# MoE routing inside a two-layer encoder: slot lists from eight one-hot products, the slot table written behind the first gathers, router products inside the output projection

## The chip, the cores and the metric

The kernel runs on one core of one Trainium2 chip. The metric is the device time of one execution in microseconds (us), median of several executions; lower is better. TensorE (PE) does the matrix products, VectorE (DVE) the elementwise work and reductions, ScalarE (ACT) activations and copies, GpSimd (POOL) some elementwise work and all indexed transfers, SyncE (SP) issues the weight transfers. The engines run side by side and wait for one another on semaphores.

## What is computed

Two layers, each a token mixer followed by a mixture of experts (MoE) on 512 tokens of width 1024. Layer 0's mixer is windowed attention, layer 1's a gated DeltaNet; the change touches only what follows the mixer. The MoE picks one of 4 groups and then the best 2 of its 8 experts for every token:

```python
g_logits = (t @ w_group) + b_group
g_prob, g_idx = lax.top_k(jax.nn.softmax(g_logits, axis=-1), 1)
e_logits = ((t @ w_expert) + b_expert).reshape(-1, N_GROUPS, EXPERTS_PER_GROUP)
e_sel = jnp.take_along_axis(e_logits, g_idx[:, :, None], axis=1)[:, 0]
e_prob, e_idx = lax.top_k(jax.nn.softmax(e_sel, axis=-1), TOP_K)
gate = g_prob * e_prob / jnp.sum(e_prob, axis=-1, keepdims=True)
...
hid = jax.nn.silu(jnp.einsum('td,edf->tef', t, w_gate)) * jnp.einsum('td,edf->tef', t, w_up)
hid = hid * combine[..., None].astype(hid.dtype)
return jnp.einsum('tef,efd->td', hid, w_down).reshape(B, S, D)
```

All is float32. An expert's three matrices are 1 MB each, 3 MB per expert, 32 experts per layer.

## The kernel before

Tokens are cut into four tiles (`TT = 4`) of 128. Every engine runs one program written out by hand; its order is the order of the calls, and semaphores tie the engines together. Around the change, in each layer:

- **Output projection** (`project_back_pe/dve/act`): for each token tile two half-width sums of 24 products (`three`), added to `x` by DVE (L315). DVE, ACT and POOL then normalise the tile (ACT L223, DVE L238, POOL L229, DVE L241 into `hn`); PE turns it (L251, `turn_pe`) so that channels lie on partitions, and ACT and DVE copy the turned tile to `ht` (L263, L277). The turn of tile t-1 stands between the two halves of tile t; that of the last tile follows the last half.
- **Router products** (`moe_pe`, L842): for all four tiles, one after another, eight products each of the tile with 36 router columns. An f32 product is two instructions, so 64 instructions in all. They begin when the last turn is done.
- **Choice** (`moe_dve`): DVE waits for the products and for `pool_c`, adds the bias (L981), and finds group and two experts by a chain of small operations that each wait for the one before (`first_max`, L972 to L977, three times). The result is two one-hot arrays `oh`. PE turns them into each token's rank within its expert (L847 to L854).
- **Table and slot lists**: DVE works out each token's row in a table in DRAM (`pos_i`, L997 to L1004). POOL writes 1,024 entries of 8 bytes there with eight indexed transfers (L738), waits until all have landed, and reads the first 64 slots of each of the 32 experts back (L743). PE turns what came (L859, L861) and DVE makes the integer lists `idx_i` from it (L1016, L1018).
- **Experts**: POOL gathers 64 token rows of an expert with one indexed transfer (L753), eight ahead (`AHEAD = 8`); PE turns them (L867), multiplies with gate and up (L875) and later with down (L884); DVE makes `hidden` (L1029) and copies the result (L1025), POOL scatters it (L760). Expert weights go through a ring of three slots (`RING = 3`) that SP refills: gate and up of a slot when L875 of its expert is done (L1924), down when L884 is (L1932).
- **POOL's own preparation** (`moe_pool`): after the four stores of `hn` to `h_rows` (L717) it writes constants (six iotas, L719 to L726) and clears the eight gather buffers (L729); the last clear raises `pool_c`. In layer 0 `masks_pool` follows, which waits until the stores of `h_rows` have landed before its last two iotas (L632, L633). DVE has a counterpart, `masks_dve`, in layer 0.

If an expert has more than 64 tokens, `late_passes` takes the rest from the table. The branch is decided at run time.

## Time and profile before

| | us |
|---|---|
| median of 3 runs | 1538.74 |
| lowest, highest | 1535.88, 1540.78 |
| span of the profiled execution | 1541.2 |
| PE busy, share of the span | 1245.0, 81% |
| PE weight loads (PEld) | 919.6, 60% |
| DVE / POOL / ACT busy | 625.7 / 508.5 / 381.3 |

The page cuts the span in 40 slices of 38.5 us and gives for each the busy share in tenths, the clock that TensorE was granted (in tenths of full speed) and the bytes moved. The two long stretches with the transfers at 9 are the expert loops of the layers. The rows farther below are from the trace of one execution, with times from the start of its span; a matmul row such as "L842 ... x64, 13.71" is a run of 64 instructions that took 13.71 us from the start of the first to the end of the last.

### The profile page before, as it was taken

Reading aid. Unit: us, or ns where it says so; the run is one execution under the profiler, and the core shown is the slowest. Engines: PE = TensorE matmul, PEld = TensorE weight load, DVE = VectorE, ACT = ScalarE, POOL = GpSimd, SP = SyncE. Lnnn points to the kernel's source line nnn. Section 1 sums busy time; section 2 is a strip of 40 time slices with the busy share of each in tenths; the row PEclk is TensorE's granted clock in tenths of the full one; section 3 lists DMA queues with packets and bytes.
Section 4 is the critical chain, followed back from the end, with each engine's and each line's share of the span. In section 5 each row is a group of like instructions: output and inputs, shape, how many; then the busy total and the mean of one; then the engine's idle time right before and its main releaser. Section 6 shows DMA issues by size and latency. Waiting matters only on the chain. (4 is left out here: it accounts for less than half of the span.)

```text
span 1541.2 us, 19154 instructions
## 1 busy us (share of the span) xinstructions
PE 1245.0 (81%) x7501; PEld 919.6 (60%) x7501; DVE 625.7 (41%) x1202; ACT 381.3 (25%) x796; POOL 508.5 (33%) x472
## 2 busy tenths in 40 slices
PE   5999989459887784798789988889979458888883
PEld 4776677435544452576688866678868434545451
DVE  4447642401111114477775576775282201111113
ACT  3325531011010012253433334332331011010010
POOL 1321000422222211045886355985440432222210
PEclk8999999579999997799999999999989579999997
DMA  6201001549999997011000130000321559999995
GB/s 207 77 34 55 1 21 60 214 167 382 396 398 387 394 411 303 0 55 55 1 1 1 55 109 2 1 1 1 110 69 55 218 190 386 404 398 392 388 408 218
DMA packets 66219, 270.65 MB, mean 176 GB/s; under 512 B 17133, under 2 KB 17389, under 8 KB 41553
## 3 DMA queue, kind: packets, MB, share of 16 engines
q1 hardware_dynamic: 52048, 246.25, 41.4%
q0 software_dynamic: 12064, 21.32, 4.1%
q10 hardware_dynamic: 2016, 1.84, 0.4%
q8 instruction: 62, 1.02, 0.3%
q14 instruction: 29, 0.23, 0.0%
HBM read 262.78 MB, written 23.35 MB: 186 GB/s over the span
## 5 line engine op out<-in xcount | busy, mean ns | idle before, releaser
L875 PE MATMUL bank<-ring,arena 128*64 128x256 f32 x2048 | 261.1, 408 | 73.6 <-issue 73.1
L875 PEld LDWEIGHTS bank<-ring,arena 128*64 128x64 f32 x2048 | 168.0, 141 | 147.7 <-issue 88.3
L760 POOL DMA_INDIRECT y_rows<-arena,idx_i x64 | 64.1, 1002 | 406.0 <-DVE arena L1025 391.2
L1318 PE MATMUL bank<-arena 128*128 128x128 f32 x1088 | 141.5, 287 | 14.9 <-DVE arena L1824 7.5
L1029 DVE TENSOR_TENSOR arena<-arena,bank 128x128 f32<-128x128 f32 x64 | 18.4, 287 | 326.8 <-ACT arena L952 321.6
L1318 PEld LDWEIGHTS bank<-arena 128*128 128x128 f32 x1088 | 132.9, 199 | 27.3 <-DVE arena L1824 11.6
L884 PE MATMUL bank<-ring,arena 128*64 128x512 f32 x512 | 123.9, 604 | 1.5 <-DVE arena L1034 1.5
L952 ACT ACTIVATE arena<-bank 128x128 f32<-128x128 f32 x64 | 17.7, 277 | 424.0 <-PE bank L875 381.3
L148 PE MATMUL bank<-ring_r,ht_r 128*128 128x512 f32 x288 | 113.5, 394 | 0.0
L1025 DVE COPY arena<-bank 128x512 f32<-128x512 f32 x64 | 44.3, 692 | 144.5 <-PE bank L884 144.5
L146 PE MATMUL bank<-ring_r,arena_r 128*128 128x512 f32 (+1 forms) x228 | 91.8, 403 | 3.4 <-DVE ring_r L170 3.4
L251 PE MATMUL bank<-ident,hn 128*128 128x128 f32 x192 | 38.5, 370 | 64.4 <-DVE hn L241 49.8
L147 PE MATMUL bank<-ring_r,arena_r 128*128 128x512 f32 x224 | 88.5, 395 | 0.0
L170 POOL TENSOR_TENSOR ring_r<-ring,ring_r 128x1024 fp32r<-128x1024 f32 x32 | 80.1, 2524 | 24.5 <-ACT ring_r L164 24.5
L867 PEld LDWEIGHTS bank<-ident,arena 64*128 64x128 f32 x512 | 61.3, 202 | 34.6 <-issue 25.1
L147 PE MATMUL bank<-ht_r,ring_r 128*128 128x512 f32 x192 | 77.9, 406 | 0.0
L867 PE MATMUL bank<-ident,arena 64*128 64x64 f32 x512 | 70.1, 278 | 9.3 <-DMA arena<-h_rows,idx_i 9.3
L251 PEld LDWEIGHTS bank<-ident,hn 128*128 128x128 f32 x192 | 33.0, 210 | 70.5 <-DVE hn L241 44.0
L1716 DVE SCALAR_TENSOR_TENSOR arena<-arena 128x512 f32<-128x512 f32 x72 | 72.8, 1011 | 2.6
L753 POOL DMA_INDIRECT arena<-h_rows,idx_i x64 | 60.7, 948 | 25.7 <-issue 18.9
L229 POOL TENSOR_TENSOR norm_s<-norm_s,mhalf 128x1 f32<-128x1 f32 x16 | 8.9, 555 | 178.1 <-DVE norm_s L238 178.1
L1629 POOL TENSOR_TENSOR arena<-ring,arena 128x512 f32<-128x512 f32 x48 | 61.9, 1310 | 6.9 <-PE bank L1318 6.9
(284 smaller groups left out, 2215.8 us busy)
## 6 DMA issues: line engine op xcount, KB each, us to landing
ring<-in_moe_w_gate SPq DMA_DIRECT2D x64, 1024.0 KB
ring<-in_moe_w_up SPq DMA_DIRECT2D x64, 1024.0 KB
ring<-in_moe_w_down SPq DMA_DIRECT2D x64, 1024.0 KB
ring<-in_gdn_w_in SPq DMA_DIRECT2D x8, 2048.0 KB
arena<-y_rows SPq DMA_DIRECT2D x16, 512.0 KB, 7.3
ring<-in_attn_w_in SPq DMA_DIRECT2D x3, 2048.0 KB
ring<-in_attn_w_out SPq DMA_DIRECT2D x2, 2048.0 KB
h_rows<-hn POOLq DMA_DIRECT2D x8, 512.0 KB, 13.9
```

The lines of the kernel that those rows point to most:

```text
L146: pe.matmul(dst, a[0], b[0], start=start, stop=False)
L147: pe.matmul(dst, a[0], b[1], start=False, stop=False)
L148: return pe.matmul(dst, a[1], b[0], start=False, stop=stop)
L170: eng.tensor_tensor(panel(n, False, True)[:, c, :], panel(n)[:, c, :], panel(n, True, True)[:, c, :].bitcast(F32), ALU.subtract).then_inc( ...
L251: last = pe.transpose(b[:, j * P:(j + 1) * P], hn[:, t, half * 4 + j::KC], ident[:, :])
L760: pool.indirect_dma_start(out=y_rows[l], out_offset=bass.IndirectOffsetOnAxis(ap=idx_i[:, 1, e:e + 1], axis=0), in_=y_out[:, e % RING, :], ...
L867: last = pe.transpose(bank[0][:, c * SLOTS:(c + 1) * SLOTS], xg[0:SLOTS, i, c::KC], ident[0:SLOTS, 0:SLOTS])
L875: last = pe.matmul(bank[1][m * SLOTS:(m + 1) * SLOTS, 0:2 * P].rearrange("p (w n) -> p w n", w=2), xgt[:, i, c * SLOTS:(c + 1) * SLOTS], w ...
L884: last = pe.matmul(bank[3][half * SLOTS:(half + 1) * SLOTS, :], hidden_t[:, i, m * SLOTS:(m + 1) * SLOTS], d[:, m, half * HALF:(half + 1) ...
L1318: last = pe.matmul(bank[b][:, h * P:(h + 1) * P], lhs(h), rhs(h), start=True, stop=True)
L1629: pool.tensor_tensor(lm[slot], lt_of(n), by_head(level[l]), ALU.mult).then_inc(g["lm"], 1)
L1716: last = dve.scalar_tensor_tensor(out=acc, in0=u_pad[:, U % 2, k:k + SEQ], scalar=conv_w[:, at:at + 1], in1=acc, op0=ALU.mult, op1=ALU.add)
```

## The change

Three things, in each of the two layers.

1. **Router products move into the projection.** Tile t-1's eight products (16 instructions) stand behind the second half of tile t; the last tile's follow its turn. DVE adds the bias tile by tile (`route_dve`, behind `norm_dve`). The logits get the first place of the arena. Before a turn reuses a bank, PE waits for the logits of the tile that used it.
2. **The slot lists are made on the chip.** For each of 2 choices and 4 tiles DVE makes a 128x128 one-hot of the token's rank (`at_slot`), and a 128x64 array `entries` that holds the token's two list values at its expert, zero elsewhere. Eight accumulating products give the 128x64 lists; DVE adds the value for an empty slot and writes `idx_i`.
3. **The table is still written**, for the late passes, but behind the first eight gathers; its read-back, the two transposes and the product on it are gone.

```diff
@@ project_back_pe
-                        turn_pe(pe, tpk + 1, t - 1)
+                        turn_routed(pe, k, tpk + 1, t - 1)
+                    if t and half:
+                        route_pe(pe, k, tpk + 1, t - 1)
             pe.wait_ge(ln["rows"], TT * (2 * k + 1) + TT)
-            turn_pe(pe, tpk + 1, TT - 1)
+            turn_routed(pe, k, tpk + 1, TT - 1)
+            route_pe(pe, k, tpk + 1, TT - 1)
+
+        def turn_routed(pe, l, k, t):
+            if t >= 2:
+                pe.wait_ge(s["logits"], TT * l + t - 1)
+            turn_pe(pe, k, t)
...
+        def route_pe(pe, l, k, t):
+            if t == 0:
+                pe.wait_ge(const_in, 16 * 13)
+            turned(pe, k, t)
+            for c in range(KC):
+                last = pe.matmul(route_bank(t)[:, 0:GROUPS + EXPERTS], ht[:, c, t * P:(t + 1) * P],
+                                 router[:, l, c, :], start=c == 0, stop=c == KC - 1)
+            last.then_inc(s["routed"], 1)
@@ project_back_dve
                 norm_dve(dve, 2 * k + 1, t)
+                if t:
+                    route_dve(dve, k, t - 1)
             turn_dve(dve, tpk + 1, TT - 1)
+            route_dve(dve, k, TT - 1)
@@ moe_pool
+                pool.iota(listed[:, k, 0, :], [[P, TT]], base=-NOBODY, channel_multiplier=1,
...
+                pool.iota(listed[:, k, 1, :], [[2 * P, TT]], base=2 * k * SEQ - NOBODY, channel_multiplier=2,
...
+            pool.iota(slot_no.rearrange("p (h j) -> p h j", h=2), [[0, 2], [1, SLOTS]], base=0, channel_multiplier=0,
...
+            pool.memset(first_of[:, 0:1], float(NOBODY))
+            o.step(pool.memset(first_of[:, 1:2], float(NOBODY + 1)))
+            pool.affine_select(out=first_of[:, 1:2], in_=first_of[:, 1:2], compare_op=ALU.is_ge, fill=float(NOBODY),
+                               base=-SLOTS, pattern=[[0, 1]], channel_multiplier=1)
             for i in range(AHEAD):
                 last = pool.memset(xg[:, i, :], 0.0)
             last.then_inc(s["pool_c"], 1)
...
-            pool.wait_ge(s["table_in"], 16 * 2 * TT + l * PER["table_in"])
-            pool.dma_start(table_sb[0:EXPERTS, :],
...
@@ moe_pe
-            for t in range(TT):
-                turned(pe, TPN[2 * l + 1], t)
-                for c in range(KC):
-                    last = pe.matmul(bank[0][:, t * 36:(t + 1) * 36], ht[:, c, t * P:(t + 1) * P],
-                                     router[:, l, c, :], start=c == 0, stop=c == KC - 1)
...
-            pe.wait_ge(s["table_sb"], 16 + l * PER["table_sb"])
...
+            for n in range(2 * TT):
+                pe.wait_ge(s["placed"], n + 1 + l * PER["placed"])
+                last = pe.matmul(bank[2][:, 0:2 * EXPERTS], at_slot[:, n // TT, n % TT, :],
+                                 entries[:, n // TT, n % TT, :], start=n == 0, stop=n == 2 * TT - 1)
+            last.then_inc(s["lists"], 1)
@@ moe_dve
+            for k in range(2):
+                dve.tensor_tensor(entries[:, k].rearrange("p t (w e) -> p t w e", w=2),
...
+            for k in range(2):
+                last = dve.tensor_tensor(masked[:, k], found, oh[:, k], ALU.mult)
+            o.step(last)
+            o.step(dve.tensor_reduce(rank_f.rearrange("p k t -> p (k t)"), masked.rearrange("p k t e -> p (k t) e"),
+                                     AX, ALU.add))
+            for k in range(2):
+                for t in range(TT):
+                    dve.tensor_scalar(at_slot[:, k, t, :], slot_no, rank_f[:, k, t:t + 1], None, ALU.is_equal
+                                      ).then_inc(s["placed"], 1)
...
+            dve.wait_ge(s["lists"], 1 + l * PER["lists"])
+            for w in range(2):
+                last = dve.tensor_scalar(idx_i[:, w, :], bank[2][:, w * EXPERTS:(w + 1) * EXPERTS],
+                                         first_of[:, w:w + 1], None, ALU.add)
+            last.then_inc(s["idx"], 1)
```

The work on `pos_i` (now two products, a reduction, an addition and a cast), the softmax terms and, in layer 0, `masks_dve` stand behind `idx_i` on DVE.

**PE, end of layer 1's projection and routing.** `ht` is the turned tile, `hn` the normalised one. Before:

```order
L251 MATMUL bank6<-ident,hn 128x128 [waits turn_act,norm_rows]
L251 MATMUL bank6<-ident,hn 128x128 x3
L251 MATMUL bank7<-ident,hn 128x128 [waits turn_dve]
L251 MATMUL bank7<-ident,hn 128x128 x3
L842 MATMUL bank0<-router,ht 128x36 [waits turn_dve,turn_act,const_in]
L842 MATMUL bank0<-router,ht 128x36 x7
```

and three more such pairs of L842. Now:

```order
L323 MATMUL bank4<-router,ht 128x36 [waits turn_dve,turn_act]
L323 MATMUL bank4<-router,ht 128x36 x7
L251 MATMUL bank6<-ident,hn 128x128 [waits turn_act,moe_logits,norm_rows]
L251 MATMUL bank6<-ident,hn 128x128 x3
L251 MATMUL bank7<-ident,hn 128x128 [waits turn_dve]
L251 MATMUL bank7<-ident,hn 128x128 x3
L323 MATMUL bank6<-router,ht 128x36 [waits turn_dve,turn_act]
L323 MATMUL bank6<-router,ht 128x36 x7
L880 MATMUL bank1<-arena,upper 128x128 [waits moe_onehots]
```

Only the last tile's products are left behind the last turn; tile 2's stand ahead of it, and those of tiles 0 and 1 farther up, between projection products.

**POOL, layer 1, from the clearing of the gather buffers to the first scatter.** Before:

```order
L726 IOTA arena 128x4
L729 MEMSET arena 128x1024 x8
L738 DMA slot_table1<-arena,pos_i 16384x2 [waits table_clear,moe_pos,moe_pool_c]
L738 DMA slot_table1<-arena,pos_i 16384x2 x7
L743 DMA arena<-slot_table1 32x128 [waits moe_table_in]
L753 DMA arena<-h_rows1,idx_i 64x1024 [waits moe_stored,moe_idx]
```

Now:

```order
L765 IOTA arena 128x128
L767 MEMSET arena 128x1
L768 MEMSET arena 128x1
L769 AFFINE_SELECT arena<-arena 128x1 [waits pool_chain]
L772 MEMSET arena 128x1024 x8
L783 DMA arena<-h_rows1,idx_i 64x1024 [waits moe_stored,moe_idx,moe_pool_c]
L783 DMA arena<-h_rows1,idx_i 64x1024 x7
L801 DMA slot_table1<-arena,pos_i 16384x2 [waits table_clear,moe_pos]
L801 DMA slot_table1<-arena,pos_i 16384x2 x7
L790 DMA y_rows1<-arena,idx_i 2048x512 [waits moe_y_copied]
```

The table's eight transfers changed places with the first eight gathers, the read-back is gone, and new constants stand ahead of the clearing.

**DVE, layer 1, from the ranks to the lists.** Before:

```order
L997 TENSOR_TENSOR arena<-bank1,arena 128x128 [waits moe_ranks]
L999 TENSOR_REDUCE arena<-bank1 128x1 [waits dve_chain]
...
L1004 CAST pos_i<-arena 128x8 [waits dve_chain]
...
L1016 CAST idx_i<-bank2 64x64 [waits moe_table_t,dve_chain]
L1018 TENSOR_SCALAR idx_i<-bank3 64x32
```

Now:

```order
L1026 TENSOR_TENSOR arena<-arena 128x256 x2
L1033 TENSOR_TENSOR arena<-bank1,arena 128x128 [waits moe_ranks]
L1033 TENSOR_TENSOR arena<-bank1,arena 128x128
L1035 TENSOR_REDUCE arena<-arena 128x8 [waits dve_chain]
L1039 TENSOR_SCALAR arena<-arena 128x128 [waits dve_chain]
L1039 TENSOR_SCALAR arena<-arena 128x128 x7
L1041 TENSOR_REDUCE arena<-bank1 128x1
L1042 CAST most_i<-arena 128x1 [waits dve_chain]
L1045 TENSOR_SCALAR idx_i<-bank2,arena 128x32 [waits moe_lists]
L1045 TENSOR_SCALAR idx_i<-bank2,arena 128x32
```

Between the ranks and `idx_i` there is no transfer any more, only eight one-hots and PE's eight products. The first operation of the choice, L1003 now, waits for `moe_logits` and `moe_pool_c`, as L981 did.

## Rows read from the trace of the kernel before

**Rows 1.** Timeline of DVE, layer 1: start us, us, engine, line, operation, [idle before]

```profile
1199.96 0.69 DVE L277 COPY ht<-bank 128x512 f32<-128x512 f32 x1 [1.97 <-PE bank L251]
...
1213.87 0.17 DVE L972 TENSOR_REDUCE arena<-arena 128x4 f32<-128x16 f32 x1
...
1223.10 0.29 DVE L997 TENSOR_TENSOR arena<-bank,arena 128x128 f32<-128x128 f32 x1 [3.64 <-PE bank L854]
...
1243.98 0.20 DVE L1018 TENSOR_SCALAR idx_i<-bank 64x32 int32<-64x32 f32 x1
```

**Rows 2.** Timeline of POOL, layer 1

```profile
1199.36 0.19 POOL L726 IOTA arena<- 128x4 f32 x1
1199.43 7.25 POOL L729 MEMSET arena<- 128x1024 f32 x8
1226.09 1.08 POOL L738 DMA_INDIRECT slot_table<-arena,pos_i  x1 [19.41 <-issue]
...
1235.18 0.97 POOL L738 DMA_INDIRECT slot_table<-arena,pos_i  x1 [0.30 <-issue]
1241.08 0.58 POOL L743 DMA_DIRECT2D arena<-slot_table  x1 [4.93 <-DMA slot_table<-arena,pos_i]
1244.99 0.99 POOL L753 DMA_INDIRECT arena<-h_rows,idx_i  x1 [3.33 <-DVE idx_i L1018]
...
1253.73 0.93 POOL L753 DMA_INDIRECT arena<-h_rows,idx_i  x1 [0.30 <-issue]
1265.41 1.02 POOL L760 DMA_INDIRECT y_rows<-arena,idx_i  x1 [10.76 <-DVE arena L1025]
```

**Rows 3.** Timeline of SP's queue, layer 1: its first load since 1196.54

```profile
1256.22 0.33 SPq L1924 DMA_DIRECT2D ring<-in_moe_w_gate  x1
```

**Rows 4.** Stretches: us, busy (count) of PE, PEld, DVE, ACT, POOL; clock, DMA share, GB/s

```profile
1216.50:1217.00 0.50, 0.00 (x0) 0.00 (x0) 0.46 (x2) 0.00 (x0) 0.00 (x0) 0.50 0.00 0
...
1226.00:1241.00 15.00, 0.00 (x0) 0.00 (x0) 0.06 (x1) 0.00 (x0) 7.92 (x8) 0.50 0.01 1
...
300.00:310.00 10.00, 0.00 (x0) 0.00 (x0) 7.45 (x38) 0.00 (x0) 7.81 (x8) 0.50 0.02 1
...
1252.00:1253.00 1.00, 1.00 (x8) 0.66 (x6) 0.00 (x0) 0.00 (x0) 0.69 (x2) 0.55 0.54 184
...
1256.00:1507.00 251.00, 214.67 (x1472) 125.23 (x1471) 35.17 (x91) 26.61 (x62) 51.91 (x53) 0.98 1.01 393
```

**Rows 5.** Timeline of PE, layer 1, at half clock

```profile
1198.05 1.88 PE L251 MATMUL bank<-ident,hn 128*128 128x128 f32 x8 [4.10 <-DVE hn L241]
1199.72 13.71 PE L842 MATMUL bank<-router,ht 128*128 128x36 f32 x64
...
1221.16 1.90 PE L854 MATMUL bank<-arena,ones 128*128 128x32 f32 x8
```

**Rows 6.** Timeline of PE in the DeltaNet, at full clock

```profile
1046.31 2.05 PE L1318 MATMUL bank<-arena 128*128 128x128 f32 x16
```

**Rows 7.** Timeline of all engines, layer 0

```profile
279.20 0.96 POOL L729 MEMSET arena<- 128x1024 f32 x1
...
287.54 0.17 DVE L972 TENSOR_REDUCE arena<-arena 128x4 f32<-128x16 f32 x1
...
291.76 0.24 POOL L632 IOTA hn<- 128x128 int32 x1 [10.67 <-issue]
...
296.76 0.29 DVE L997 TENSOR_TENSOR arena<-bank,arena 128x128 f32<-128x128 f32 x1 [3.64 <-PE bank L854]
...
320.01 1.00 POOL L753 DMA_INDIRECT arena<-h_rows,idx_i  x1 [3.48 <-DVE idx_i L1018]
...
332.49 0.29 DVE L1029 TENSOR_TENSOR arena<-arena,bank 128x128 f32<-128x128 f32 x1 [13.33 <-ACT arena L952]
```

**Rows 8.** DMA queues of the page: packets, MB, share of 16 engines

```profile
q1 hardware_dynamic: 52048, 246.25, 41.4%
q0 software_dynamic: 12064, 21.32, 4.1%
```

More of the change, by code:

```diff
@@ L37 @@
 ROWS = PASSES * SLOTS
-NOBODY = 60000.0
+NOBODY = 60000
 RING = 3
@@ L662, in build @@
         ml = Layout()
+        logits = ml.take(TT, GROUPS + EXPERTS)
         xg = ml.take(AHEAD, D)
@@ L669, in build @@
         y_in = [cut(2 * D * t, 2, D) for t in range(TT)]
-        logits = ml.take(TT, GROUPS + EXPERTS)
         oh_g = ml.take(TT, GROUPS)
@@ L681, in build @@
         payload = ml.take(TT, 2 * 2)
-        table_sb = ml.take(SLOTS * 2)
+        listed = ml.take(2, 2, TT)
+        entries = ml.take(2, TT, 2 * EXPERTS)
+        slot_no = ml.take(P)
+        first_of = ml.take(2)
+        at_slot = ml.take(2, TT, P)
+        rank_f = ml.take(2, TT)
         pos_f = ml.take(2, TT)
@@ L695, in build @@
         late_step = [sem(f"late_step{l}") for l in range(2)]
-        PER = dict(most=1, stored=16 * TT, logits=1, pool_c=1, dve=2, exp_g=1, exp_e=1, onehots=1, ranks=1, pos=1,
-                   table_in=16 * 2 * TT, table_sb=16, table_t=1, idx=1, combined=TT)
+        PER = dict(most=1, stored=16 * TT, routed=TT, logits=TT, pool_c=1, dve=2, exp_g=1, exp_e=1, onehots=1,
+                   ranks=1, pos=1, table_in=16 * 2 * TT, placed=2 * TT, lists=1, idx=1, combined=TT)
         PER.update({n: EXPERTS for n in ("st", "turned", "xgt", "up", "silu", "hidden", "hid_turned", "hid_t",
@@ L766, in moe_pool @@
                 gather(e)
+            pool.wait_ge(s["pos"], 1 + l * PER["pos"])
+            pool.wait_ge(table_clear, 32)
+            for k in range(2):
+                for t in range(TT):
+                    pool.indirect_dma_start(
+                        out=tables[l], out_offset=bass.IndirectOffsetOnAxis(ap=pos_i[:, k, t:t + 1], axis=0),
+                        in_=payload[:, t, 2 * k:2 * k + 2], in_offset=None,
+                        bounds_check=EXPERTS * ROWS - 1, oob_is_err=False).then_inc(s["table_in"], 16)
             for e in range(EXPERTS):
@@ L837, in moe_pe @@
             n0 = MOE_AT[l]
-            pe.wait_ge(const_in, 16 * 13)
-            for t in range(TT):
-                turned(pe, TPN[2 * l + 1], t)
-                for c in range(KC):
-                    last = pe.matmul(bank[0][:, t * 36:(t + 1) * 36], ht[:, c, t * P:(t + 1) * P],
-                                     router[:, l, c, :], start=c == 0, stop=c == KC - 1)
-            last.then_inc(s["logits"], 1)
             pe.wait_ge(s["onehots"], 1 + l * PER["onehots"])
@@ L856, in moe_pe @@
             last.then_inc(s["ranks"], 1)
-            pe.wait_ge(s["table_sb"], 16 + l * PER["table_sb"])
-            for w in range(2):
-                last = pe.transpose(bank[2][0:SLOTS, w * EXPERTS:(w + 1) * EXPERTS],
-                                    table_sb[0:EXPERTS, w::2], ident[0:EXPERTS, 0:EXPERTS])
-            last = pe.matmul(bank[3][SLOTS:P, 0:EXPERTS], table_sb[0:EXPERTS, 1::2], ident[0:EXPERTS, 0:EXPERTS],
-                             start=True, stop=True)
-            last.then_inc(s["table_t"], 1)
+            for n in range(2 * TT):
[3 more added lines that the diff above has]
+            last.then_inc(s["lists"], 1)
             def turn_rows(i):
@@ new lines, in moe_dve @@
+            dve.wait_ge(s["ranks"], 1 + l * PER["ranks"])
+            found = bank[1][:, 0:TT * EXPERTS].rearrange("p (t n) -> p t n", t=TT)
+            for k in range(2):
[3 more added lines that the diff above has]
+                                     AX, ALU.add))
+            for k in range(2):
+                for t in range(TT):
+                    dve.tensor_scalar(at_slot[:, k, t, :], slot_no, rank_f[:, k, t:t + 1], None, ALU.is_equal
+                                      ).then_inc(s["placed"], 1)
@@ new lines, in moe_dve @@
+            last.then_inc(s["idx"], 1)
+            for k in range(2):
+                last = dve.tensor_tensor(masked[:, k], oh[:, k], base.unsqueeze(1).to_broadcast([P, TT, EXPERTS]),
+                                         ALU.mult)
+            o.step(last)
+            o.step(dve.tensor_reduce(pos_f.rearrange("p k t -> p (k t)"), masked.rearrange("p k t e -> p (k t) e"),
+                                     AX, ALU.add))
+            o.step(dve.tensor_tensor(pos_f, pos_f, rank_f, ALU.add))
@@ L2010, in _ @@
             pool.iota(dist, [[-1, BAND]], base=P, channel_multiplier=1, allow_small_or_imprecise_dtypes=True)
-            last = pool.memset(nobody[:, :], NOBODY)
+            last = pool.memset(nobody[:, :], float(NOBODY))
             o.step(last)
```

35 lines of the change are left out of this document (14 added, 21 removed).

## The prediction, made before the changed kernel was run

> **What bounds the kernel now.** I read the slices of the page first: transfers are full in the two expert loops and empty between, so the loops are bound by the weight stream. The stretch table confirms it for layer 1: from 1256 to 1507 us the DMA share is 1.01 at 393 GB/s [rows 4]. Next I asked what sets the start of that stream. SP's queue issues nothing between 1196.54, when the three-slot ring has been given all it can take, and 1256.22, when the first expert's gate-and-up products end [rows 3]; the transfers are at 0.00 from 1216.5 [rows 4]. So for some 40 us the weight transfers stand still, waiting for the first expert. **Every microsecond by which the first expert comes earlier moves the whole stream**, until the first refill would fall before 1216.5, and since the loop's length is the stream's, the end of the layer moves by as much. Last I followed the timelines backwards from the first gather (1244.99) [rows 2]: lists 1243.98 [rows 1], read-back 1241.08, eight table transfers 1226.09 to 1236.15 and 4.93 us of landing [rows 2], ranks at 1223.10, choice from 1213.87, router products 1199.72 to 1213.43 [rows 1, 5]. All in line, with PE at half clock. Layer 0 has the same shape: choice 287.54, ranks 296.76, gather 320.01 [rows 7].
>
> **Router products, what is added.** Three tiles' products move ahead of the last turn. The 64 instructions took 13.71 us at half clock, 0.214 us each [rows 5]. In the projection PE runs at full clock and is never idle. No row shows these there. If they follow the clock they take half, 0.107; f32 products of 128 columns take 2.05/16 = 0.128 at full clock [rows 6]. Both have the same 128 wide operand to load, so I take 0.12: 1.9 us for a tile. Tiles 0 and 1 lie on PE's path: **3.8 us later per layer** (3.4 at 0.107, 6.8 at 0.214). Tile 2 lies in the 4.10 us in which PE waits for the last `hn` [rows 5] and costs nothing; without that cover it would be 1.9. The new wait for `logits` ahead of a turn is for a tile two turns back, long done.
>
> **Router products, what is removed, and what is late next.** The last tile's products can start when `ht` is complete, 1200.65 [rows 1]. 16 instructions as in 13.71/64 = 3.4 us plus the bias, about 0.3, gives logits at 1204.4 instead of 1213.87, 9.4 us less, were nothing else waited for. But L1003 also waits for `pool_c`, which comes with the last clearing on POOL: 1199.43 + 7.25 = **1206.68** [rows 2], and POOL starts on it only after the last `hn`, so all of it moves with the 3.8 us. POOL now does more ahead of it: four iotas of 128x4 (the last of before takes 0.19, and what follows starts 0.07 after its start [rows 2]: 0.3), one iota of 128x128 (0.24 [rows 7]), two memsets and an affine select of 128x1 with a wait between (no row; by the two iotas 0.07 to 0.24 each, and the wait lets nothing overlap: 0.45). I take 1.0 us (0.7 to 1.4). So the choice starts at 1206.68 + 3.8 + 1.0 + 0.05 = 1211.5 in layer 1, and in layer 0, where the clearing ends at 279.20 + 0.96 = 280.16 [rows 7], at 285.0. Against 1213.87 and 287.54 that is **only 2.4 and 2.5 us earlier**; the other 3.2 us of the move go into a new wait of DVE for POOL. From here to the ranks nothing changes: 9.23 us [rows 1], 9.22 [rows 7]. `entries` (two operations of 128x256) fit into the 3.64 us in which DVE waits for the ranks [rows 1].
>
> **From the ranks to the first gather.** Before: 1244.99 - 1223.10 = 21.9 us [rows 1, 2], in layer 0 320.01 - 296.76 = 23.25 [rows 7]. Now: two products with the one-hots (0.5 with the second overlapping, from 0.29 each), a reduction over 256 elements (0.45, between the 0.29 for 128 and twice that), the first `at_slot` (0.29): 1.3 us with the waits. Then PE: 8 products are 16 instructions at 0.21 us at half clock plus the tail of the last, 3.6 us (L854 had 8 in 1.90 [rows 5], twice that is 3.8); the seven other one-hots at 0.2 to 0.29 each come faster than PE's 0.43 per product. Then two writes of `idx_i` of 0.20 and the 0.81 from there to POOL's gather (1243.98 + 0.20 to 1244.99) [rows 1, 2]. Sum 1.3 + 3.6 + 0.1 + 0.4 + 0.8 = **6.2 to 6.3 us** (5.5 if the clock is up, 8 if each product waits for its one-hot). `pos_i` now stands behind `idx_i` and costs nothing ahead of it.
>
> **The sum.** First gather, layer 1: 1211.5 + 9.2 + 6.3 = 1227.0 instead of 1245.0, 18.0 us. Layer 0: 285.0 + 9.2 + 6.3 = 300.5 instead of 320.0, 19.5 us. Together 37.5. It is all kept: the ring is full at 1216.5 + 3.8 = 1220, and the first refill at 1256.2 - 18 = 1238. The stores of `h_rows` must have landed before a gather: POOL passed that wait at 291.76 in layer 0 [rows 7], so 295.6 now against 300.5. The profiled span of 1541.2 becomes 1503.7; the median was 2.5 below the span, so **1501**.
>
> **What is moved on POOL and DVE.** The eight gathers take from lists to last end 1254.66 - 1244.18 = 10.5 us, the table's eight transfers 1236.15 - 1226.09 = 10.1 [rows 2]: POOL is free 20.9 us after the lists. The first scatter came at 1265.41, 21.2 after them [rows 2]. It just fits, and a late one has the three `y_out` buffers behind it, the gather behind it eight experts. In layer 0 DVE has `pos_i` (2 us), the softmax terms (1) and the masks (7.5 to 8, most of the 7.45 us that DVE is busy from 300 to 310 [rows 4]) between lists and first `hidden`, 11 us; before, DVE idled 13.33 us there, from the lists to 332.49 [rows 7]. Hidden, by 2 us.
>
> **The table writes beside the stream.** Standing alone, eight table transfers used 0.01 of the DMA engines in 15 us [rows 4], 0.15 us: nothing. Beside the stream no row shows them. A packet of POOL's queue took on average 0.041 x 1541 x 16 / 12064 = 0.084 us of an engine [rows 8]; 64 pieces for each of 16 engines at that are 5.4 us per layer, an upper bound for pieces of 8 bytes. I take 0.2 and keep 10.8 for the range. The Trainium skill, "DMA: Bandwidth & Descriptors", "Queues, rings and completion order", says an engine goes round the queues that have work, a packet at a time; by that the table's small packets alternate with weight packets instead of queueing behind them. By that rule the loss is their own time, and only the landing of the table gets long, for which nothing waits; the trace has no such stretch.
>
> **Rivals.** (a) *The clock.* The granted clock is 0.50, 1.2 GHz, from the router products on, and rises to 2.4 GHz inside the first gate-and-up products (0.55 in the stretch from 1252) [rows 4]. Ranks and list products now lie closer together: if they bring it up, the list products take half, 1.7 us less, and the gate-and-up products up to 1.5 less: 3 us per layer, 1495. Against: some 4 us of idle PE stay ahead of the first expert. The Trainium skill, "TensorE: Matmul & The Clock Gate" (Why this matters for your kernels), has a matmul engine that idles between bursts fall back to the low clock; by that (a) is less likely, and its chance below is kept small. (b) *POOL does not hold the choice* (the clearing is not what DVE waits for): the 3.2 us per layer come as gain, 1495. The code has the wait, so it would need a faster clearing. (c) *The added work costs more*: router products at 0.214, one-hots paced by waits, the table at its upper bound; 3 to 10 us more, 1504 to 1512. (d) *No change*: the stream was not held by the ring, and starting earlier only makes it wait later; the 40 idle us speak against it. 1539. (e) *Slower*: the 8-byte writes now fall into the stream and hold each of 16 DMA engines. To eat 37.5 us over two layers each of the 128 pieces per engine must cost 0.29 us, 3.5 times the average packet of that queue; at 0.4 it would be 51 - 37.5 = 14 us slower, 1552.
>
> **How the numbers follow.** Forecast (1497 to 1506, centre 1501): 0.66. (a) or (b): 0.15. (c): 0.14. (d): 0.02. (e): 0.03. The range takes the ends of (a) and the cheap half of (c): 1494 to 1509. A difference under 0.3%, 4.6 us, cannot be told from none here. Faster by more: 0.95, within: 0.02, slower by more: 0.03.
>
> **What would show it.** The choice's first reduction on DVE idles before starting, and POOL's clearing ends just ahead of it (right), or the bias addition does (wrong). Ranks to first gather 6 to 6.5 us. Projection 3.8 us longer per layer, the routed tiles 1.9 each. The next load on SP's queue in layer 1 at 1238 instead of 1256.2. DMA share still 1.01 over the loop and its length 251 us: if it grew, the table writes or the gathers were paid there. What would make it wrong most easily: a loop that is no longer set by the stream's start.

## The result, and the profile after

The changed kernel took 1520.09 us (median of 4, 1516.42 to 1522.82) against 1537.31 for the kernel before on the same chip. The ratio is 0.9884, with a 95% interval of 0.9860 to 0.9907: faster by some 18 us, where 37.7 had been forecast, and outside the range. The profiled execution spans 1521.2 us, against 1541.2.

I read it in the order of the prediction's steps. First the router products, on PE's timeline (start us, us, engine, line, operation, [idle before]): the last product of the projection, the third tile's router products at full clock, and the last turn.

```profile
1188.39 0.39 PE L148 MATMUL bank<-ring_r,ht_r 128*128 128x512 f32 x1
1188.62 1.87 PE L323 MATMUL bank<-router,ht 128*128 128x36 f32 x16
1192.88 1.16 PE L251 MATMUL bank<-ident,hn 128*128 128x128 f32 x8 [2.39 <-DVE hn L241]
```

A tile costs 1.87 us (1.9 had been taken). The last turn starts at 1192.88 against 1198.05 [rows 5]; layer 0 had by then gained 9.0 us (600.56 - 591.56, rows below), so it stands 3.8 us later within its layer, as forecast. The start of the choice, on DVE in layers 0 and 1, and POOL's clearing in layer 1:

```profile
280.44 0.19 DVE L329 TENSOR_TENSOR arena<-bank,router_b 128x36 f32<-128x36 f32 x1 [3.79 <-PE bank L323]
284.24 0.17 DVE L1003 TENSOR_REDUCE arena<-arena 128x4 f32<-128x16 f32 x1 [3.60 <-POOL arena L772]
...
1198.56 0.20 DVE L329 TENSOR_TENSOR arena<-bank,router_b 128x36 f32<-128x36 f32 x1 [3.78 <-PE bank L323]
1202.42 0.17 DVE L1003 TENSOR_REDUCE arena<-arena 128x4 f32<-128x16 f32 x1 [3.67 <-POOL arena L772]
```

```profile
1195.22 7.17 POOL L772 MEMSET arena<- 128x1024 f32 x8
1217.98 1.04 POOL L783 DMA_INDIRECT arena<-h_rows,idx_i  x1 [15.59 <-DVE idx_i L1045]
```

The logits are there at 280.6, and the choice waits 3.60 us more for POOL, as forecast (3.2); it starts at 284.24 where [rows 7] had 287.54. From the ranks to the first gather, DVE and PE of layer 0 and the first gather on POOL:

```profile
293.52 0.49 DVE L1033 TENSOR_TENSOR arena<-bank,arena 128x128 f32<-128x128 f32 x2 [2.97 <-PE bank L887]
...
298.55 0.41 DVE L1045 TENSOR_SCALAR idx_i<-bank,arena 128x32 int32<-128x32 f32 x2 [2.11 <-PE bank L892]
```

```profile
294.84 3.68 PE L892 MATMUL bank<-arena 128*128 128x64 f32 x16 [1.36 <-DVE arena L1039]
```

```profile
299.87 1.04 POOL L783 DMA_INDIRECT arena<-h_rows,idx_i  x1 [4.33 <-issue]
```

299.87 - 293.52 = 6.35 us (6.2 to 6.3 forecast), and the first gather comes at 299.87 (300.5 forecast), 20.1 us earlier than at [rows 7]. So far every step holds. Now the expert loops, each taken from the first refill (the first weight load that waits for the first expert's products) to the first read of the expert outputs: SP's queue, these two rows, before

```profile
332.18 0.33 SPq L1924 DMA_DIRECT2D ring<-in_moe_w_gate  x1
...
600.56 3.85 SPq L1065 DMA_DIRECT2D arena<-y_rows  x8
...
1520.37 3.80 SPq L1065 DMA_DIRECT2D arena<-y_rows  x8
```

and after:

```profile
311.84 0.33 SPq L1970 DMA_DIRECT2D ring<-in_moe_w_gate  x1
...
591.56 3.88 SPq L1111 DMA_DIRECT2D arena<-y_rows  x8
...
1229.47 0.33 SPq L1970 DMA_DIRECT2D ring<-in_moe_w_gate  x1
...
1501.96 3.77 SPq L1111 DMA_DIRECT2D arena<-y_rows  x8
```

Layer 0's loop was 600.56 - 332.18 = 268.4 us and is 279.7; layer 1's was 1520.37 - 1256.22 [rows 3] = 264.2 and is 272.5. The first refill comes 332.18 - 311.84 = 20.3 us earlier in layer 0 and 1256.22 - 1229.47 = 26.8 in layer 1, of which 9.0 are layer 0's gain. **The starts bring 20.3 us in layer 0 and 17.8 in layer 1, and the loops give 11.3 and 8.3 back.** Where in the loop, the stretches of layer 0 after show (columns as in [rows 4]):

```profile
316.00:341.00 25.00, 19.29 (x133) 10.43 (x131) 3.52 (x9) 2.59 (x6) 9.26 (x10) 0.94 1.01 243
341.00:366.00 25.00, 22.24 (x145) 12.83 (x141) 3.47 (x9) 2.59 (x6) 3.94 (x4) 0.93 1.02 394
```

The DMA engines are as full as ever (1.01), but for 25 us they move 243 GB/s instead of 394. That alone is 25 x (1 - 243/394) = 9.6 us. The eight table transfers were issued from 310.19 to 320.3. The DMA queues of the 33 us from 312 and of the 33 us from 400 (packets, MB, share of 16 engines) say who holds the engines:

```profile
q1 hardware_dynamic: 989, 7.27, 88.2%
q0 software_dynamic: 699, 0.86, 8.3%
```

```profile
q1 hardware_dynamic: 1650, 12.02, 93.0%
q0 software_dynamic: 602, 0.90, 8.4%
```

It is not POOL's queue (q0) that takes more: 8.3% against 8.4. The weight packets themselves take longer: 88.2/7.27 = 12.1% for a MB against 93.0/12.02 = 7.7. The loss stands in another queue's row than the work that causes it.

### The profile page after: what moved, and what is told of

It is laid out like the page before. It is cut to its first block and busy times, and to the rows that moved or that the text cites. A ratio compares the mean times of both kernels' runs of the same rounds, so it can differ in the third digit from the quotient of the medians.

```text
span 1521.2 us, 19250 instructions
## 1 busy us (share of the span) xinstructions
PE 1245.8 (82%) x7525; PEld 922.7 (61%) x7525; DVE 632.5 (42%) x1232; ACT 381.8 (25%) x796; POOL 510.4 (34%) x486
## 5 line engine op out<-in xcount | busy, mean ns | idle before, releaser
L906 PE MATMUL bank<-ring,arena 128*64 128x256 f32 x2048 | 265.2, 413 | 89.7 <-issue 86.9
L906 PEld LDWEIGHTS bank<-ring,arena 128*64 128x64 f32 x2048 | 174.4, 143 | 161.8 <-issue 109.4
L1364 PEld LDWEIGHTS bank<-arena 128*128 128x128 f32 x1088 | 133.0, 200 | 27.3 <-DVE arena L1870 11.1
L983 ACT ACTIVATE arena<-bank 128x128 f32<-128x128 f32 x64 | 17.8, 278 | 442.4 <-PE bank L906 442.4
L783 POOL DMA_INDIRECT arena<-h_rows,idx_i x64 | 61.9, 968 | 38.8 <-issue 23.2
```

Source lines behind the costliest of these rows:

```text
L906: last = pe.matmul(bank[1][m * SLOTS:(m + 1) * SLOTS, 0:2 * P].rearrange("p (w n) -> p w n", w=2), xgt[:, i, c * SLOTS:(c + 1) * SLOTS], w ...
L1364: last = pe.matmul(bank[b][:, h * P:(h + 1) * P], lhs(h), rhs(h), start=True, stop=True)
```

## The experiments

Beside the change, fourteen more kernels ran, each beside the kernel before on its own chip; "brings" is (1 - ratio) x 1538 us. Differences between kernels are taken from this column; each value has an interval of 2.5 to 6 us either way.

| kernel | median us | ratio (interval) | brings us |
|---|---|---|---|
| the change | 1520.1 | 0.9884 (0.9860-0.9907) | 17.8 |
| b1: table only in the late branch | 1501.5 | 0.9746 (0.9729-0.9763) | 39.1 |
| e2: twice the table transfers | 1549.8 | 1.0060 (1.0042-1.0077) | -9.2 |
| e3: table ahead of the gathers | 1530.7 | 0.9939 (0.9921-0.9956) | 9.4 |
| e4: pieces of 512 bytes | 1528.0 | 0.9922 (0.9905-0.9939) | 12.0 |
| r1: reads instead of writes | 1525.0 | 0.9890 (0.9867-0.9914) | 16.9 |
| e5: pieces 512 bytes apart | 1521.7 | 0.9882 (0.9854-0.9909) | 18.1 |
| e6: one behind each of 8 scatters | 1502.0 | 0.9751 (0.9735-0.9767) | 38.3 |
| e9: two in a row, four times | 1508.9 | 0.9811 (0.9779-0.9843) | 29.1 |
| e10: four in a row, twice | 1519.7 | 0.9890 (0.9861-0.9918) | 16.9 |
| e8: eight in a row, behind the third scatter | 1525.6 | 0.9892 (0.9855-0.9928) | 16.6 |
| e7: four in a row ahead of the stream | 1511.9 | 0.9818 (0.9782-0.9853) | 28.0 |
| b3: b1, router products behind the last turn | 1509.7 | 0.9795 (0.9754-0.9836) | 31.5 |
| b2: b1, tell to DVE ahead of the clearing | 1499.1 | 0.9729 (0.9711-0.9747) | 41.7 |
| b5: e6, half of the clearing later | 1502.2 | 0.9752 (0.9719-0.9786) | 38.1 |

**Are the table writes the cause?** b1 issues them only where they are needed, in the branch for experts with more tokens than slots:

```diff
-            for k in range(2):
-                for t in range(TT):
-                    pool.indirect_dma_start(out=tables[l], ...)
             for e in range(EXPERTS):
                 scatter(e)
 ...
             def ready():
+                for k in range(2):
+                    for t in range(TT):
+                        pool.indirect_dma_start(out=tables[l], ...)
```

> The changed kernel with the table's eight transfers moved into the branch of the late passes, which this input does not take, so that no 8-byte piece is written beside the stream. Theory A (the table's small writes slow the weight stream): the loop from the first refill to the first read of y_rows goes from 279.7 us back to 268.4 in layer 0 and from 272.5 to 264.2 in layer 1, first gathers stay where they are (299.9 in layer 0): about 1520 - 19.6 = 1500.5 us. Rival B (the stream is slow because the first experts start closer to the fill of the ring, whatever is written): unchanged loops, 1520.

1501.5 us. Its SP queue shows layer 0's loop at 582.96 - 313.33 = 269.6 us (268.4 before the change) and layer 1's at 264.1 (264.2), and the stretch in which the change had moved 243 GB/s is full:

```profile
316.00:341.00 25.00, 25.00 (x183) 14.38 (x181) 3.82 (x10) 3.10 (x8) 5.95 (x6) 1.00 1.01 393
```

The whole miss hangs on these sixteen transfers, and without them the kernel takes what was predicted. Twice as many (e2, the second eight into a table of their own), and all of them ahead of the gathers (e3):

```diff
             for e in range(AHEAD):
                 gather(e)
             for k in range(2):
                 for t in range(TT):
                     pool.indirect_dma_start(out=tables[l], ...)
+            for k in range(2):
+                for t in range(TT):
+                    pool.indirect_dma_start(out=twins[l], ...)
```

> The changed kernel with every table transfer written a second time, to a second table that nobody reads: 2048 pieces per layer instead of 1024. Theory A: each piece costs the stream the same, the loops grow by another 11.3 and 8.3 us, about 1540 us (and some more if the ten further us on POOL's queue delay the first scatters). Rival B: unchanged, 1520 to 1523.

```diff
+            for k in range(2):
+                for t in range(TT):
+                    pool.indirect_dma_start(out=tables[l], ...)
             for e in range(AHEAD):
                 gather(e)
-            for k in range(2):
-                for t in range(TT):
-                    pool.indirect_dma_start(out=tables[l], ...)
```

> The changed kernel with the table's eight transfers ahead of the first eight gathers, in the pause of the weight stream, still without read-back. Theory A: the first gather comes later by the 1.3 us for pos_i and eight times 1.28 us, 11.5 us in each layer, and the loops take 268.4 and 264.2 again: 1520 + 23 - 19.6 = 1523.5 us. Rival B: the gathers late and the loops still long, 1543. Rival C (the cost moves with the writes because they are slow by themselves): loops short but the gathers wait, also near 1523; the loop lengths tell A from B, and the landing time of the table tells A from C (about 5 us standing alone).

e2: 1549.8, by the ratios 27 us over the change for as many transfers more (48 over b1 for 32 of them, 1.5 us each). e3: 1530.7, 7 over what was expected, with a loop of 596.93 - 327.76 = 269.2 us, the short one. So in the pause they cost the loop nothing. The 7 us fit the gathers, which stand behind the table in the queue: the first landed 8.6 us after its issue instead of 3.9, 4.7 us in a layer.

**Size, direction, place?** e4 writes pieces of 512 bytes, r1 reads the 8 bytes from the cleared table into a spare tile and does not write them, e5 puts each 8-byte piece 512 bytes from the next; e4 and e5 leave the real table as cleared.

```diff
-                        out=tables[l], out_offset=bass.IndirectOffsetOnAxis(ap=pos_i[:, k, t:t + 1], axis=0),
-                        in_=payload[:, t, 2 * k:2 * k + 2], in_offset=None,
+                        out=wide[l], out_offset=bass.IndirectOffsetOnAxis(ap=pos_i[:, k, t:t + 1], axis=0),
+                        in_=at_slot[:, k, t, :], in_offset=None,
```

> The changed kernel with pieces of 512 bytes instead of 8, at rows of 512 bytes in a scratch table, the same 1024 per layer at the same places; the content is not used. If the price is that of a piece smaller than some size (theory A1), it falls to the bytes alone, 0.5 MB at 393 GB/s, 1.3 us per layer: 1503. If it is the price of any scattered piece (A2), loops as in the changed kernel plus those bytes: 1520 to 1523.

```diff
-                        out=tables[l], out_offset=bass.IndirectOffsetOnAxis(ap=pos_i[:, k, t:t + 1], axis=0),
-                        in_=payload[:, t, 2 * k:2 * k + 2], in_offset=None,
+                        out=probe[:, k * TT + t, :], out_offset=None, in_=tables[l],
+                        in_offset=bass.IndirectOffsetOnAxis(ap=pos_i[:, k, t:t + 1], axis=0),
```

> The table is written only inside the late branch, which these inputs never enter (with all writes in that branch the kernel took 1501.5 us, the changed kernel 1520.1). Where the changed kernel writes its eight table transfers of 128 pieces of 8 bytes, this one reads as many pieces of 8 bytes from the cleared table, at the same positions, into a spare tile that nothing uses. Number, size, place and moment of the pieces are the same, only the direction differs. Theory P (each small piece costs the engines its turn, whatever the direction): 1520, with the loop of layer 0 some 10 us longer than 269.5. Theory W (what costs is writing small pieces to DRAM): 1501 to 1505.

```diff
-        tables = ... [EXPERTS * ROWS, 2]       (written)
+        wide = ... [EXPERTS * ROWS * 64, 2]    (written)
-            dve.tensor_copy(pos_i[:, :, :], pos_f)
+            dve.tensor_scalar(pos_i[:, :, :], pos_f, 64.0, None, ALU.mult)
```

> As the changed kernel, but each 8-byte piece goes to a scratch table whose rows lie 512 bytes apart (positions times 64), so the 1024 pieces of a layer are spread over 1 MB instead of 16 KB. The table that the late branch would read stays as cleared; the branch is not entered. Theory N (neighbouring pieces are written into the same few places of DRAM and wait for one another): most of the 18.6 us between 1520.1 and 1501.5 goes, 1501 to 1508. Theory P (a price for each piece wherever it lands; the 512-byte pieces, 512 bytes apart, cost no less): 1520, perhaps 1528 as with those.

1528.0, 1525.0 and 1521.7: none frees the time. Neither that they are writes, nor their 8 bytes, nor that they land close together is the cause. But in these three and in e2 most of the time goes in another way, which I had not expected. In layer 0 their loops are short (e4: 592.72 - 323.42 = 269.3); it is the first refill that is late. In e4, on PE, on ACT, on SP's queue, and on POOL its last table transfer:

```profile
306.52 6.08 PE L907 MATMUL bank<-ring,arena 128*64 128x256 f32 x32 [0.82 <-ACT arena L977]
312.53 1.09 PE L899 MATMUL bank<-ident,arena 64*128 64x64 f32 x8
```

```profile
323.43 0.28 ACT L984 ACTIVATE arena<-bank 128x128 f32<-128x128 f32 x1 [15.75 <-remote]
```

```profile
323.42 0.33 SPq L1971 DMA_DIRECT2D ring<-in_moe_w_gate  x1
```

```profile
320.06 0.98 POOL L802 DMA_INDIRECT wide_table<-arena,pos_i  x1 [0.30 <-issue]
```

PE's gate-and-up products end at 312.6, and ACT and SP, which both wait for them and for nothing else, go on only at 323.4, after the last table transfer. The same wait ends at 321.38 in r1, at 322.20 in e5, and at 335.45 in e2, whose sixteen transfers end at 332.15. In the changed kernel it ended at once, at 311.84, and the stream was slow instead. The signal is raised late, not noticed late: in e4 the trace's list of semaphore updates has that semaphore rise at 323.41, and the one that PE's turn of the next rows raises, due 1.0 us later, at 323.50.

Layer 1 shows the two forms side by side. The signal is late by 8.5 us in e4, 7.7 in e5, 4.9 in r1 and 9.1 in e2, and the loops behind it are long as well: 267.5, 267.8, 269.8 and 278.9 us against b1's 264.1. There the signal does not wait for the end of the row: in r1 SP goes on at 1233.97 and the last transfer is issued at 1236.88. From the first gather to the first read of the outputs, which holds both forms, a layer takes 281.5 and 275.5 us in b1; the change is 10.2 and 8.5 over that, e4 10.5 and 11.9, e5 12.0 and 10.7, r1 8.6 and 10.7, e2 24.4 and 23.2. So the two forms together come to about the same loss whatever the split: 8.5 to 12.0 us for a row of eight.

**How many in a row?** e6 issues the same eight transfers one behind each of the first eight experts' scatters:

```diff
             for e in range(EXPERTS):
                 scatter(e)
                 if e + AHEAD < EXPERTS:
                     gather(e + AHEAD)
+                if e < 2 * TT:
+                    k, t = divmod(e, TT)
+                    pool.indirect_dma_start(out=tables[l], ...)
```

> As the changed kernel, but the eight table transfers are not issued together after the first gathers: one stands behind the scatter and gather of each of the first eight experts. If each piece has its price whenever the stream is full: 1520. If the price comes from the burst (eight transfers at the moment when the empty stream starts again): 1501 to 1510. The first refill of layer 0 should come at 312 to 313.5 us in both cases.

1502.0: nothing lost that can be seen (0.9751 against b1's 0.9746, 0.8 us, and the intervals allow 4), with the same 2048 pieces beside the same stream. **It is not a price of the piece; it is one of the row.** Then four in a row ahead of the stream (e7, the other four not issued), eight in a row inside the running stream (e8, `if e == 2:` in e6's place), and two and four in a row (e9 behind scatters 1, 3, 5 and 7, e10 behind 2 and 9, counted from 0).

> As the changed kernel, but four of the eight table transfers stand behind the first gathers; the other four are issued in the late branch, which these inputs do not enter. Theory P (a price for each piece or transfer): half of the 18.6 us between the changed kernel (1520.1) and the one without table writes (1501.5) goes: 1510.8. Theory B (a price of the burst as such, since the same eight transfers, one behind each of eight scatters, cost nothing, 1502.0): it stays near 1520, if four transfers already make the burst, or falls to 1502, if they don't.

> As the changed kernel, but the eight table transfers are issued together behind the third expert's scatter, some 16 us after the first refill, when the weight stream is full again. Theory B1 (eight transfers in a row cost the stream some 9 us wherever they fall): 1520. Theory B2 (they cost only where they fall on the first expert and the first refills, before the stream is full): 1502 to 1504. The gathers run eight experts ahead and three buffers stand behind the scatters, so the 10.4 us of POOL's time are hidden in both cases.

> As the changed kernel, but the eight table transfers are issued two in a row, behind the scatters of the second, fourth, sixth and eighth expert. With one behind each of eight scatters it took 1502.0 us, with eight in a row behind the third scatter 1525.6. If the price grows with how many follow one another, past some length: 1502 to 1504. If only a lone transfer is free and every further one of a row costs 1.2 us (23.6/2 layers/8, rounded down for the first): 4 of 8 transfers pay, 1511.

> As the changed kernel, but the eight table transfers are issued four in a row, behind the third and the tenth scatter. If the price is one of each transfer in a row: as eight in a row, 1520 to 1526. If it starts only behind a certain length of the row, beyond four: 1502 to 1504. Four in a row ahead of the stream cost 10.4 us over two layers (1511.9).

Over b1: 0.8 us for one at a time, 10.0 for two in a row, 22.1 for four, 22.5 for eight, 11.1 for e7's four. By how many table transfers stand directly behind another one (0, 8, 12 and 14 over both layers) that is 0, 1.3, 1.8 and 1.6 us each. A lone transfer behind a scatter and a gather is free within the noise, each further one costs; with intervals of that size the three prices can't be told apart. e6 changes two things at once, the count in a row and the time between transfers (7 us instead of 1.3), and the scatters and gathers beside the row are indirect transfers too. Whether the count, the rate or the number under way at once is what matters was not separated. e7's first refill comes late (316.44, 17.1 us behind its first gather instead of 12), as in e4, e5 and r1. e8 shows that the first expert has no part in it, and also when the loss comes. The table transfers were issued from 338.68 on, 1.3 us apart; the stretches (from 338, from 346 and from 366 us):

```profile
338.00:346.00 8.00, 8.00 (x60) 4.44 (x57) 1.27 (x3) 0.86 (x2) 6.17 (x7) 1.00 1.03 383
346.00:366.00 20.00, 12.67 (x63) 5.94 (x62) 2.32 (x6) 1.62 (x4) 7.19 (x9) 0.81 0.96 146
366.00:400.00 34.00, 26.52 (x169) 16.01 (x171) 3.53 (x9) 2.59 (x6) 6.33 (x7) 0.86 1.02 378
```

For 8 us nothing happens, then the stream falls to 146 GB/s for 20 us, with the engines at 0.96: 20 x (1 - 146/394) = 12.6 us. PE, SP's queue and ACT in that stretch:

```profile
345.44 1.09 PE L899 MATMUL bank<-ident,arena 64*128 64x64 f32 x8
353.24 0.33 SPq L1971 DMA_DIRECT2D ring<-in_moe_w_gate  x1
353.25 0.28 ACT L984 ACTIVATE arena<-bank 128x128 f32<-128x128 f32 x1 [12.32 <-remote]
```

The gate-and-up products end at 345.5, where PE's turns begin, and SP and ACT go on 7.7 us later. So the late signal is no matter of the empty stream: it comes in the running one too, and in the same stretch as the slow packets. In e8's layer 1 it is 7.7 us again, in e10 some 2.2 in each layer. The kernels without a row (b1, b2, b3, b5, e6) and the one before have none over 1.2 us, but neither have the change, e3 and e9: the late signal comes only with a row, and not with every one.

**The router part by itself.** b3 is b1 with all router products again in one row behind the last turn.

```diff
                         pe.wait_ge(ln["rows"], TT * (2 * k + 1) + t)
-                        turn_routed(pe, k, tpk + 1, t - 1)
-                    if t and half:
-                        route_pe(pe, k, tpk + 1, t - 1)
+                        turn_pe(pe, tpk + 1, t - 1)
             pe.wait_ge(ln["rows"], TT * (2 * k + 1) + TT)
-            turn_routed(pe, k, tpk + 1, TT - 1)
-            route_pe(pe, k, tpk + 1, TT - 1)
+            turn_pe(pe, tpk + 1, TT - 1)
+            turned(pe, tpk + 1, TT - 1)
+            for t in range(TT):
+                route_pe(pe, k, tpk + 1, t)
```

> One part of the change undone: all router products stand again behind the last turn, in one row at half clock, and not inside the projection. The table is written only in the late branch, as in the kernel that took 1501.5 us, so that the loops keep what the start gives. By the prediction's steps the choice then starts 13.2 us behind the last copy of the turned rows instead of waiting for POOL's clearing, which ends 3.8 us earlier: in layer 0 about 2.5 to 3.3 us later than with the products inside, so 5 to 7 us over two layers: 1506.5 to 1508.5. Rival: inside the projection they cost as much as they bring (8 x 1.9 us of PE, the wait for POOL), 1501.5.

1509.7, 7.5 us over b1 by the ratios (b3's interval is 6 us either way). The traces bear the size out: the first gather of layer 0 comes at 305.29 against b1's 301.51, 3.8 us, and that of layer 1 at 1213.95 against 1207.34, 6.6 us, of which 3.0 were there at layer 0's end. So of the 39 us that b1 brings, this part is some 7.5, and the lists, with the table out of the way, are the rest.

**The new wait for POOL.** b2 is b1 with the tell ahead of the clearing:

```diff
-            pool.affine_select(out=first_of[:, 1:2], ...)
+            last = pool.affine_select(out=first_of[:, 1:2], ...)
+            last.then_inc(s["pool_c"], 1)
             for i in range(AHEAD):
                 last = pool.memset(xg[:, i, :], 0.0)
-            last.then_inc(s["pool_c"], 1)
```

> Table written only in the late branch (1501.5 us), and POOL tells the choice on DVE that its constants are ready before it clears the eight buffers of the gathered rows, instead of after; the gathers wait for the clearing. If the wait for POOL held the choice by 3.6 us in each layer, as the trace of the changed kernel says: choice at 280.8 instead of 284.2 us in layer 0, first gather at 297.5 to 298, end 7 us earlier, 1494.5. If something else would hold it (a slower DVE beside the clearing, the bias addition later than I read, the stores of the rows, which had landed at 295 us): 1497 to 1501.

1499.1, 2.6 us below b1 by the ratio where 7 were expected. DVE begins the choice as soon as the logits are there, and then stops in its midst; in b2, DVE, and POOL's clearing with what follows it:

```profile
280.12 0.17 DVE L1004 TENSOR_REDUCE arena<-arena 128x4 f32<-128x16 f32 x1
280.32 0.17 DVE L1006 TENSOR_TENSOR arena<-arena 128x16 f32<-128x16 f32 x1
...
281.25 2.66 DVE L1015 TENSOR_SCALAR arena<-arena 128x16 f32<-128x16 f32 x1
283.94 0.29 DVE L1017 TENSOR_TENSOR arena<-arena 128x128 f32<-128x128 f32 x1
```

```profile
276.41 7.17 POOL L773 MEMSET arena<- 128x1024 f32 x8
```

One tensor_scalar over 128x16 takes 2.66 us instead of 0.17, until 283.9; POOL's clearing ends at 283.58. The six operations ahead of it, four of them tensor_tensor with both inputs in SBUF, ran at full speed beside the same clearing. The Trainium skill, "GPSIMD Engine Reference" (Specifications), has POOL share its SBUF interfaces with DVE and names two kinds of DVE instruction that contend: those in a 2-port mode and those with two SBUF inputs. This trace bears out the first, if the tensor_scalar is of that kind; of the second it shows no slowing beside a clearing, which reads nothing. Beside a POOL operation that reads SBUF no row shows it. Of the 3.6 us of the wait only 1.1 were to be had: from the end of the bias addition to the end of the choice (L1026 in b1) it is 8.8 us against 9.9. b5 takes the clearing out of the way instead, in e6:

```diff
-            for i in range(AHEAD):
+            for i in range(AHEAD // 2):
                 last = pool.memset(xg[:, i, :], 0.0)
             last.then_inc(s["pool_c"], 1)
 ...
             for e in range(AHEAD):
+                if e == AHEAD // 2:
+                    for i in range(e, AHEAD):
+                        last = pool.memset(xg[:, i, :], 0.0)
+                    o.step(last)
                 gather(e)
```

> A version meant to beat both. The table transfers stand one behind each of the first eight scatters (1502.0 us), and POOL clears only four of the eight buffers of gathered rows before it tells the choice on DVE; the other four it clears between the fourth and the fifth gather. When the tell came ahead of the whole clearing, the choice began 3.6 us earlier but one 128x16 operation on DVE took 2.66 us instead of 0.17, until POOL's clearing had ended, and only 1.1 us per layer were left. If that was DVE held up by POOL's clearing, then here, where the clearing ends at about 280.0 us in layer 0, just as the last logits are there (280.0), the choice keeps 3.5 us per layer: 1495. If it was something else in the choice, 1499 to 1500.

1502.2, no gain over e6, although the reason given for b2's stop was right. In b5, DVE's same operation and POOL:

```profile
281.71 0.17 DVE L1018 TENSOR_SCALAR arena<-arena 128x16 f32<-128x16 f32 x1
```

```profile
276.88 3.62 POOL L772 MEMSET arena<- 128x1024 f32 x4
```

The operation is back at 0.17 us and the choice starts 0.1 us behind the logits. The first refill of layer 1 stands at 1209.66 against e6's 1215.73, 6.1 us earlier, but the loop to the first read of the outputs takes 1479.03 - 1209.66 = 269.4 us against 1479.97 - 1215.73 = 264.2. Of the 6.1 us 5.1 are given back; in layer 0 the refill is 1.9 us earlier and the loop 2.0 longer. The last four gathers now go out beside the first refills, and the first 20 us of the stream move 345 GB/s in b5 against 389 in e6:

```profile
1210.00:1230.00 20.00, 19.49 (x145) 11.73 (x144) 3.22 (x9) 2.60 (x6) 8.18 (x9) 1.00 1.00 345
```

```profile
1216.00:1236.00 20.00, 19.56 (x143) 11.41 (x144) 3.23 (x9) 2.94 (x8) 5.99 (x6) 1.00 0.97 389
```

That is 20 x (1 - 345/389) = 2.3 of the 5.1 us; that the gathers' row causes it, as the table's did, is argued, not shown, and where the rest goes stays open.

## Why the prediction missed, step by step

- **What bounds the kernel**: right. The start of the stream set the end: in b1, which starts as the prediction said, the time is 1501.5 against 1501. That it meets to 0.5 us is partly luck: the kernel before alone has medians from 1536.7 to 1540.6 us on the chips used.
- **Router products, added and removed**: right. 1.87 us a tile (1.9), choice at 284.24 (285.0), held by POOL for 3.60 us (3.2). Rival (b) named the clearing as the thing to make faster; b2 shows that its 3.2 us a layer were not to be had by the tell alone, since DVE then stops at 281.25 for 2.5 us.
- **Ranks to first gather**: right, 6.35 us (6.2 to 6.3). The clock stayed at half as forecast: the lists' 16 instructions took 3.68 us (3.6), so rival (a) fell.
- **Sum of the starts**: right, 20.3 and 17.8 us at the first refill (19.5 and 18.0).
- **"It is all kept"**: wrong. 11.3 and 8.3 us, 19.6 together, went in the loops, which accounts for the miss of 19.
- **"The table writes beside the stream ... I take 0.2"**: this is the step that failed. It measured 21 us over both layers (b1 against the change), some 10 a layer; by the loops of the changed kernel it is 11.3 and 8.3. The upper bound of 5.4 was made from the mean packet of POOL's queue, that is, from the time which these transfers hold an engine under their own name. The profile after has that time unchanged (8.3% against 8.4), and the loss in the packets of the weights. A bound from the causing queue's own row could not hold it. The pause of before, with eight such transfers at a share of 0.01 [rows 4], said even less, since no other queue ran beside them.
- **The rule that was weighed there** (the Trainium skill, "DMA: Bandwidth & Descriptors", "Queues, rings and completion order": an engine goes round its queues a packet at a time) promised a loss of the small packets' own time. In the running stream this case measured 9.6 us in 25 instead, so the measurement decides. It does not say that the rule is false, but that turn-taking by itself gives too small a loss here; what gives the rest was not found.
- **Rival (e)** had the mechanism's place right, and a chance of 0.03; its price is 0.15 us per piece in these units (19.6/128) where it needed 0.29 to turn the sign. e6 shows that its form, a price for each of 128 pieces per engine, was wrong all the same: the same pieces, one transfer at a time, cost nothing that can be seen. **Rival (c)**, 3 to 10 us more, had the right kind of miss and too small a size: its upper end was 1512. **Rival (d)**, no change, falls with b1.
- **POOL's time, masks, landing**: right. The first scatter came at 321.86, 10.0 us behind the first refill.

## What to carry to other kernels

Where work is moved out of a pause into a stretch in which a queue runs full, price it by what it does to that queue, not by its own time: no row of the pause shows it, so the bound has to be wide. Small indirect transfers that nobody waits for are issued one at a time between other work (e6: nothing lost) or not at all until they are needed (b1), never in a row beside a full stream. And when a wait is lifted, look what the engine does next beside the work that it no longer waits for.

## What the runs showed of the hardware that I had not expected

- Eight indirect transfers of 128 pieces in a row slow a weight stream from 394 to between 146 and 243 GB/s for 20 to 25 us, in e8 with a lag of 8 us, while the DMA share stays at 0.96 to 1.01. Singly, 7 us apart, they do nothing that can be seen (e6). What in the machine is used up by the row was not found; it is none of the direction, the 8 bytes or the pitch.
- In e2, e4, e5, r1, e7, e8 and e10 a signal of PE to ACT and SP was raised late while such a row was under way or had just been issued: in layer 0 by 5 to 22 us at the first expert (e7 5.2, r1 9.5, e4 10.8, e5 11.1, e2 22.3), in layer 1 by 2.6 to 9.1, and in the running stream by 7.7 (e8) and 2.2 (e10). In layer 0 of the first five it came only after the last issue of the row, in layer 1 of all five before the last issue had ended. Waits and products are those of the changed kernel, where it came at once. Why it is the one or the other is open.
- A tensor_scalar on DVE stood still for 2.5 us beside POOL's clearing, until that ended, while tensor_tensor and tensor_reduce beside the same clearing took their usual 0.17 us (b2).
